# Raw weights of the last two query heads loaded after an accumulating transfer, the transfers issued at other places, ScalarE's negation ahead of its copies of scores

## The reference

```
q  = (h @ peer_wq).reshape(B, T, 8, 256)          # 8 heads, two halves of 128
s1 = q1 @ sub_keys1.T ;  s2 = q2 @ sub_keys2.T     # 128 scores per half, token and head
v1, i1 = top_k(s1, 16) ; v2, i2 = top_k(s2, 16)
cand   = v1[i] + v2[j]                             # 256 pairs, expert i1*128 + i2
top_s, pos = top_k(cand, 16) ; gate = softmax(top_s)
out = sum over the 16 x 8 picked experts of gate * gelu(h . peer_u[e]) * peer_v[e]
```

## Time and profile before

| | |
|---|---|
| median of 3 runs | 985.12 us (984.2 to 985.66) |
| profiled execution | 982.17 us |
| its span | 980.4 us |
| PE busy | 960.9 us (98%) |
| DVE busy | 751.0 us (77%) |
| ACT busy | 465.6 us (47%) |
| POOL busy | 193.8 us (20%), all before 325 us |
| accumulating transfers | 4 of 1 MB, issued at 165.94, 179.28, 188.25 and 199.31 us |
| PE idle before the products of heads 4, 5, 6, 7 | 0.51, 2.64, 0, 0.82 us |

### The profile page before, as it was taken

One profiled execution on the slowest core, in us unless ns is written; L12 is line 12 of the kernel. 1 busy time (PEld: TensorE's weight loads), 2 busy tenths in 40 slices (PEclk: granted clock), 3 DMA queues, 4 the chain that ended last, 5 costly groups with the idle time before them and its releaser, 6 DMA issues.

```text
span 980.4 us, 16912 instructions
## 1 busy us (share of the span) xinstructions
PE 960.9 (98%) x5616; PEld 844.3 (86%) x5616; DVE 751.0 (77%) x1385; ACT 465.6 (47%) x718; POOL 193.8 (20%) x234
## 2 busy tenths in 40 slices
PE   7999999899999999999999999999999999999998
PEld 7998899898999888888888888888888888888886
DVE  5799767998988887777767777777767777777766
ACT  5566545433777534434444444434444444434442
POOL 4074227986887100000000000000000000000000
PEclk9999999999999999999999999999999999999999
DMA  8543129845222776555555545555555555555554
GB/s 264 171 129 122 52 88 332 199 99 166 80 56 59 244 239 226 173 199 187 185 200 176 209 173 204 179 195 190 181 204 176 208 173 201 184 189 196 176 209 150
DMA packets 70164, 172.57 MB, mean 176 GB/s; under 512 B 6752, under 2 KB 35552, under 8 KB 69616
## 3 DMA queue, kind: packets, MB, share of 16 engines
q1 hardware_dynamic: 68080, 167.47, 50.6%
q0 software_dynamic: 576, 4.19, 2.1%
q10 hardware_dynamic: 1472, 0.44, 0.2%
HBM read 163.16 MB, written 4.72 MB: 171 GB/s over the span
## 4 chain that ended last, share of the span: by engine, by line
PE 75%; DVE 1%; issue 0%; DVEq 0%; POOL 0%
PE psum L1851 36%; PE psum L1831 20%; PE psum L1834 10%; PE psum L1790 6%; PE psum L1797 2%; PE psum L1721 1%; DVE big L1129 0%; PE psum L1480 0%; DVE big L1273 0%; DVE big L1140 0%; PE psum L1778 0%; DVEq L102 0%; DVE big L1175 0%; POOL big L1376 0%; DVE big L1171 0%
## 5 line engine op out<-in xcount | busy, mean ns | idle before, releaser
L1851 PE MATMUL psum<-rr 128*128 128x512 f32 x1536 | 369.1, 391 | 0.0
L1851 PEld LDWEIGHTS psum<-rr 128*128 128x128 f32 x1536 | 288.0, 188 | 59.1
L1831 PE MATMUL psum<-h_all,rr 128*128 128x512 f32 x856 | 306.6, 392 | 0.0
L1195 DVE TENSOR_TENSOR rr<-raw,rr 128x1024 fp32r<-128x1024 f32 x109 | 133.6, 1226 | 144.9 <-ACT rr L757 144.9
L757 ACT ACTIVATE rr<-raw 128x1024 fp32r<-128x1024 f32 x109 | 115.5, 1060 | 270.2 <-PE psum L1851 270.2
L1834 PE MATMUL psum<-h_all,rr 128*128 128x256 f32 x856 | 221.9, 280 | 0.0
L1831 PEld LDWEIGHTS psum<-h_all,rr 128*128 128x128 f32 x856 | 160.6, 188 | 32.2 <-DVE rr L1134 0.6
L1834 PEld LDWEIGHTS psum<-h_all,rr 128*128 128x128 f32 x856 | 160.8, 188 | 8.2
L645 ACT ACTIVATE rr<-raw 128x1024 fp32r<-128x1024 f32 x107 | 113.6, 1062 | 66.2 <-DMA raw<-in_peer_u_dram 62.1
L1134 DVE TENSOR_TENSOR rr<-raw,rr 128x1024 fp32r<-128x1024 f32 x107 | 130.6, 1221 | 3.9 <-ACT rr L645 1.8
L1181 DVE TENSOR_TENSOR rr<-psum,picks 128x2048 fp32r<-128x2048 f32 x32 | 72.4, 2288 | 9.3 <-PE psum L1790 7.6
(11 more groups left out here) (205 smaller groups left out, 952.5 us busy)
## 6 DMA issues: line engine op xcount, KB each, us to landing
raw<-in_peer_u_dram SPq DMA_DIRECT2D x128, 512.0 KB, 4.1
raw<-in_peer_v_dram SPq DMA_DIRECT2D x128, 512.0 KB, 3.6
big<-in_w_in_dram SPq DMA_DIRECT2D x10, 1024.0 KB, 6.1
big<-in_peer_wq_dram SPq DMA_DIRECT2D x8, 1024.0 KB, 6.2
big<-in_w_out_dram SPq DMA_DIRECT2D x4, 1024.0 KB, 5.2
rr<-big POOLq DMA_DIRECT2D x4, 1024.0 KB, 8.2
up_kept<-gel SPq DMA_DIRECT2D x20, 128.0 KB, 3.6
gel<-up_kept SPq DMA_DIRECT2D x20, 128.0 KB, 3.8
```

The source lines that it names most:

```text
L1195: dve.tensor_tensor(v_sp[s][:, 1, :], v_raw[s], f(v_sp[s][:, 0, :]), ALU.subtract).then_inc(v_lo, 1)
L1831: return pe.matmul(both, ut[s][:, 0, k, :], ht[:, :, k, :], start=(k == 0), stop=(k == DK - 1))
L1851: i = pe.matmul(psum[:, 4 + 2 * t + n, :], g_sp[:, s, x, t * P:(t + 1) * P], v_sp[s][:, y, n * 512:(n + 1) * 512], start=(first and m == 0 ...
```

## The change

SPq no longer loads chunk WQ0+6 right after WQ0+5. Chunks WQ0+6 and WQ0+7 are loaded after `keep_early(0)` and `keep_early(1)`, each behind a new wait for the accumulating transfer of head 4 and of head 5. On ACT the negation of chunk WQ0+h+2 stands ahead of `keep_s(h)`, directly behind the split. On POOL the transfer of head 5 is issued ahead of the wait for `d_match` and the two products, where head 4's already was, and that of head 6 between the two products. That of head 7 stays behind both. What is computed is unchanged.

```diff
             for e in range(3):
                 load_ring(e)
             load_w(WQ0 + 5)
-            load_w(WQ0 + 6)
             for e in range(EARLY):
                 keep_early(e)
-                if e == 1:
-                    load_w(WQ0 + 7)
+                if e < 2:
+                    sp.wait_ge(ld_neg[e], 16)
+                    load_w(WQ0 + 6 + e)
...
                 c = WQ0 + h + 2
                 if c in SPLIT_Q[2:]:
                     split_w(c)
-                keep_s(h)
                 if c in ADDED_Q:
                     act.wait_ge(w_hi, c - 1)
                     act.activation(w_sp[:, w_slot(c), 1], f(w_sp[:, w_slot(c), 0]), ACT.Copy, scale=-1.0).then_inc(q_neg, 1)
+                keep_s(h)
...
                 pool.wait_ge(p_cide, g + 1)
-                if g == 0:
-                    add_low(0)
+                if g < 2:
+                    add_low(g)
                 pool.wait_ge(d_match, g + 1)
                 tiles = 2 if g < PH - 1 else 1
                 for t in range(tiles):
+                    if g == 2 and t == 1:
+                        add_low(2)
                     i = pool.tensor_tensor(eqs[:, s, t], ...)
...
                 if g == 0:
                     candidates(1)
-                elif g < len(ADDED_Q):
-                    add_low(g)
+                elif g == 3:
+                    add_low(3)
```

## The result

The changed kernel takes 987.94 us, the median of 9 runs (986.87 to 989.54), against 985.13 us for the kernel before in the same runs: ratio 1.0035, 95% interval 1.0021 to 1.0049. Run again on another chip it was 1.0044 (1.0027 to 1.0062). It is slower by 2.8 to 4.5 us where 2.3 us less were forecast. Its profiled execution took 987.44 us; that of before, 982.17, lay 2.95 under its median, so the two traces differ by 5.3 us, more than the medians do. The stage begins 0.99 us sooner in the trace after (PE's first products of a split head at 146.30 against 147.29); I take that off where times are compared.

What follows compares the result with a forecast made beforehand. DVE and POOL end the heads' stage, held through ACT's copies and PE by accumulating transfers. Picks 2.3 us sooner (POOL's last wait 2.25, DVE's row 2.4) gave 985.12 - 2.3 = 982.8 us; range 981.4 to 985.2.

Steps and rivals of the forecast that it cites:

- What bounds the kernel: In the heads' stage, up to 3.97 us of PE waits for transfers lie behind 3.40 us of DVE waits.
- What follows the picks: Everything after the turned picks on PE was to move 2.3 us sooner and otherwise take the same time.
- Head 4: Its transfer issued at 164.75, landing at 172.3 to 173.65; PE's wait of 0.51 us goes.
- The negation's cost: On ACT, copies of heads 2 to 5 stand behind a 1.91 us negation; 1.7 of head 5's 3.15 us kept.
- Head 5's transfer: Issued by POOL at 175.1 against 179.28, landing after 8.5 us at 183.6; head 5's products start 3.15 us sooner.
- hidden anyway: Rival (0.11): head 5's transfer lands some 2 us later than forecast, best_keys(5) gains nothing, time 985.1.
- The loads: WQ0+6 and WQ0+7 on SPq land after 6.5 us, at 179.7 and 190.2, hidden by 0.9 to 1.1 us.
- company: Rival (0.18): loads beside the next accumulations cost 1.3 us, DVE's gain at the end is 1.5, time 983.6.
- late load, slower: Rival (0.09): WQ0+7 lands late for ACT's split; slower from a 9.7 us load on, 3.3 us lost at 13.0.
- turns among queues: Each DMA engine takes turns among its queues, whoever issued, so company would slow both sides.
- PE's products: Products of heads 4 to 7 were to start at 174.4, 184.65, 194.6 and 204.6; head 4's took 5.94 us.
- What would show it wrong: Splits of WQ0+6 or WQ0+7 released by a load, accumulations over 9 us, picks at 239.5, or changed times past the picks.

Runs made afterwards that it cites:

- e6: Changed kernel with the loads of WQ0+6 and WQ0+7 in their old places and the negation ahead of the copies at heads 2 and 3 only: ratio 0.9972.
- e9: The changed kernel run again unaltered, as a base for later runs: 987.41 us, ratio 1.0044 to the kernel before.
- e5: Changed kernel with the load of WQ0+6 back in its old place, WQ0+7 still behind head 5's transfer: ratio 0.9979 to the kernel before.
- e11: Changed kernel with the load of WQ0+6 cut to 8 of 128 partitions: 981.98 us, ratio 0.9992 to the kernel before.
- e8: Changed kernel with the load of WQ0+7 replaced by one of the same bytes in pieces of 4 KB instead of 1 KB: ratio 1.0028.
- e10: Changed kernel with the load of WQ0+7 cut to 8 of 128 partitions: 983.39 us, ratio 1.0006 to the kernel before.
- e12: Changed kernel with head 6's transfer issued behind both products again: ratio 1.0017 to the kernel before.
- e2: Kernel before with only the loads of WQ0+6 and WQ0+7 moved behind the accumulating transfers: ratio 1.0038.

## Why the prediction was wrong

*What bounds the kernel* was right: DVE ends the stage, held by copies of scores, these by PE, and PE by the transfers. With PE's waits nearly gone (e6: 0.37, 0, 0.31 and 0.21 us) the picks come at 236.02 against 239.53, 2.3 us sooner once the 1.17 by which e6's stage begins sooner (146.12) are taken off. What follows the picks I moved unchanged; in the changed kernel's trace it took 0.9 us longer (985.6 - 243.84 against 980.4 - 239.53), but in e9, the same kernel, 740.4 against 740.9, so that this is the scatter of single executions.

*Head 4* was right: the issue to 0.1 us, the landing 0.3 past my latest, PE's wait gone. *The negation's cost* was about right: DVE waited 0.73 us at head 4 where I had 0.7, none at head 3 where I had 0.4.

*Head 5's transfer* is the first step that failed. I gave it "its own 8.5 us" and at most 8.9. That 8.5 already held a wait for WQ0+7, asked for 2.97 us ahead, and the new place had WQ0+6 1.65 us and a ring block 1.23 us ahead. With only a ring block it takes 7.6 to 7.7 us (e5, e11), with a load and a ring block ahead 11.0 to 12.0 (changed kernel, e8, e9, e10, e12). The products' gain of 3.15 us became 1.17. Against the rival *hidden anyway* I had held that a landing 11 us after issue had not been seen; that is what came.

*The loads* are the step that failed in size and decided. I took "6.5 us" and a slack of 0.9. The load of WQ0+7 was asked for 2.9 us later than I had it (185.61 against 183.7 - 0.99) and took 12.2. I had priced company at 1.3 us, the difference of 8.9 and 7.6 in the earlier trace rows; but in both of these what was ahead (WQ0+6, a ring block) was nearly through when the transfer began, so the rows showed the tail of a queue and not two transfers side by side. The rival *late load, slower* (0.09), with the point of 9.7 us and a price of 3.3 at 13.0, is what happened. That 12.2 us on its line give 2.5, where 2.8 were measured, is luck: the load was asked for 2.9 us later than that line has it and its split wanted it 3.5 us later (193.14 + 0.49 + 0.99 against 191.1), and the two traces differ by 5.3. I had its path, a late load in front of ACT's work, but not its cause, and gave it too little chance, since I judged it by the median of 5.9 over all loads. On turns among queues, for which I cited the Trainium skill, "DMA: Bandwidth & Descriptors", section "SWDGE vs HWDGE vs iDMA", the runs agree only in part: in 190 to 194 us of the changed kernel the two queues moved 94 and 95 packets, turn by turn, which gave the transfer 0.77 MB and the load 0.10; in e2 and e8 the one that came later moved nothing in 4 us. There the measurement decides. Company did slow both sides, as I had put it, but by 3.7 and 5.7 us (11.3 against 7.6 for head 6's transfer, 12.2 against 6.5 for the load), not by 1.3.

*PE's products* I moved with unchanged length. After the idle 2.26 us head 5's took 7.47 instead of 5.92, at a lower granted clock. These are four stretches of the changed kernel (us; busy us of PE, PEld, DVE, ACT, POOL; clock, DMA share, GB/s):

```profile
180.00:184.00 4.00, 3.38 (x20) 2.75 (x18) 3.32 (x10) 3.97 (x4) 3.87 (x16) 1.00 1.03 219
184.00:188.00 4.00, 2.36 (x14) 2.36 (x15) 3.83 (x26) 0.65 (x4) 3.92 (x4) 0.80 0.42 64
188.00:192.00 4.00, 4.00 (x29) 4.00 (x29) 3.88 (x27) 0.00 (x0) 4.00 (x10) 0.78 1.02 247
192.00:196.00 4.00, 4.00 (x29) 3.74 (x28) 1.49 (x2) 0.60 (x1) 3.87 (x8) 1.00 1.01 258
```

Read by single microseconds, the clock of this trace is 1.00 up to 186 us, 0.50 from 187 to 189, the level of 1.2 GHz, and 1.00 again, the level of 2.4 GHz, from 190 on. In the trace of before the idle 2.64 us at the same place left the clock at 1.00.

*What would show it wrong* named the right rows: the split released by a load, and accumulations over 9 us.

## What to carry to other kernels

A transfer's time in a trace holds what was ahead of it; before one is moved, read the bytes per queue, microsecond by microsecond, and add up the engines' time of all that is asked for in the new place, in the order of asking, and in either order where the gap is under a microsecond. A load put "behind" a transfer is put in front of the next one: what counts is the gap between them, and here about three microseconds of it (e5, where WQ0+6 also went back, against the changed kernel) separated a gain of 0.2% from a loss of 0.4%. A wait on a landing makes one late transfer ask late for the next.

## What the runs showed of the hardware

An accumulating transfer of 1 MB within the on-chip memory needed 6.9 to 7.8 us from issue to landing in the cases where it had least company; it moved 0.19 MB per us with all 16 engines busy. Once it moved, a plain load beside it got 0.10 MB in 4 us (changed kernel) or none (e8); where the load moved first, the accumulation got none in 4 us (e2). Why an accumulation is that slow, and how the engines choose, these runs do not show.

PE's clock fell after some idle times and not after others: after 2.05 (e11), 2.26, 2.49, 2.64 (e12, head 5), 2.72, 2.75 (e8), 3.02 (e9, head 7), 3.29, 3.45 (changed kernel, head 7), 3.86 and 4.33 us the next products took 7.3 to 8.3 us; after 1.82 (e2), 1.85 (e8, head 7), 2.13 (e5), 2.64 (before) and 2.74 us (e12, head 6) 5.9. What tells these apart is open. No run was made for the clock's cost by itself, but the traces of e5 and e11 nearly give it, since there head 6's products start after much the same wait (e5's row, then e11's):

```profile
196.85 5.93 PE L1693 MATMUL psum<-h_all,rr 128*128 128x256 f32 x48 [2.13 <-DMA rr<-big]
...
196.46 7.42 PE L1693 MATMUL psum<-h_all,rr 128*128 128x256 f32 x48 [2.05 <-DMA rr<-big]
```

The clock in 196 to 200 us was 1.00 in e5 and 0.60 in e11. DVE waited 1.55 and 3.03 us for the copies of head 6, and the picks came at 238.57 and 239.67. So 1.5 us of slower products cost about 1.1 us at the picks, in one execution of each.
